# A four-layer decoder kernel on one core: its opening in another order, with zeros multiplied while the input is loaded

## The reference

```python
def _rmsnorm(x, g):
    return x * lax.rsqrt(jnp.mean(jnp.square(x), axis=-1, keepdims=True) + RMS_EPS) * g

def _mla(x, positions, w_dq, q_norm, w_uq, w_dkv, kv_norm, w_ukv, w_o):
    cq = _rmsnorm(x @ w_dq, q_norm)                     # 1024 -> 384
    q = (cq @ w_uq).reshape(b, s, h, NOPE + ROPE)       # rope on the last 64
    ckv = x @ w_dkv                                     # 1024 -> 256 + 64
    c_kv = _rmsnorm(ckv[..., :KV_LORA], kv_norm)
    k_pe = _rope(ckv[..., KV_LORA:], positions, theta)
    kv = (c_kv @ w_ukv)
    ...

# differential attention, second layer:
lam = exp(sum(lq1 * lk1)) - exp(sum(lq2 * lk2)) + lambda_init
```

## Time and profile before

| | us |
|---|---|
| median of 3 runs | 1593.34 |
| the runs | 1593.21 to 1595.19 |
| the profiled execution | 1595.48 |
| its span, first to last instruction | 1593.7 |

### The profile page before, as it was taken

The page is one execution under the profiler, slowest core; times in us unless marked ns, Lnnn a source line. Parts: engine busy times, 40 slices in busy tenths (PEclk is TensorE's granted clock), DMA queues, the critical chain, the costliest instruction groups (busy, mean ns, idle before and its releaser), DMA issues.

```text
span 1593.7 us, 20708 instructions
## 1 busy us (share of the span) xinstructions
PE 1557.3 (98%) x8570; PEld 1338.0 (84%) x8570; DVE 1077.0 (68%) x1390; ACT 752.9 (47%) x874; POOL 18.5 (1%) x77
## 2 busy tenths in 40 slices
PE   7999999999999999999999999999999999999997
PEld 6878888799888888888888888887888888788886
DVE  6777656868766567655777665577555868965557
ACT  4734444357254353544455254444444365444542
POOL 1000000000000000000000000000000000000000
PEclk9999999999999999999999999999999999999999
DMA  8446655553465565666474655546555562475551
GB/s 265 133 142 210 199 190 185 191 178 108 151 219 186 193 198 189 187 194 198 143 230 133 205 186 190 185 159 224 194 190 185 157 210 94 132 237 185 185 189 49
DMA packets 198444, 285.97 MB, mean 179 GB/s; under 512 B 9287, under 2 KB 167055, under 8 KB 198351
## 3 DMA queue, kind: packets, MB, share of 16 engines
q1 hardware_dynamic: 194943, 272.20, 52.6%
q0 software_dynamic: 3264, 11.93, 2.3%
q10 hardware_dynamic: 144, 0.52, 0.1%
HBM read 283.58 MB, written 1.05 MB: 179 GB/s over the span
## 4 chain that ended last, share of the span: by engine, by line
PE 81%; DVE 12%; ACT 3%; issue 1%; DMA 1%; SPq 0%; DVEq 0%; ACTq 0%
PE ps L397 39%; PE ps L426 25%; PE ps L430 13%; DVE wlo L293 2%; PE ps L449 2%; ACT whi L288 2%; DVE x L529 1%; DVE res L526 1%; DVE stats L503 1%; DVE res L500 1%; DVE xt L488 1%; DVE nt L518 1%; DMA raw<-in_mla_w_dq 1%; DMA raw<-in_w_in_mlstm 1%; PE ps L1577 1%
## 5 line engine op out<-in xcount | busy, mean ns | idle before, releaser
L293 DVE TENSOR_TENSOR wlo<-raw,whi 128x2048 fp32r<-128x2048 f32 (+2 forms) x259 | 576.7, 2256 | 232.6 <-ACT whi L288 231.4
L288 ACT ACTIVATE whi<-raw 128x2048 fp32r<-128x2048 f32 (+2 forms) x262 | 483.0, 1879 | 20.3 <-DMA raw<-in_w_in_mlstm 4.8
L397 PE MATMUL ps<-whi,yt 128*128 128x512 f32 (+1 forms) x1472 | 462.4, 387 | 1.7 <-DVE wlo L293 1.0
L426 PE MATMUL ps<-xt,whi 128*128 128x512 f32 x1728 | 431.8, 392 | 0.0
L426 PEld LDWEIGHTS ps<-xt,whi 128*128 128x128 f32 x1728 | 314.7, 189 | 58.2
L397 PEld LDWEIGHTS ps<-whi,yt 128*128 128x128 f32 x1472 | 275.5, 189 | 56.8 <-DVE wlo L293 2.3
L397 PE MATMUL ps<-wlo,yt 128*128 128x512 f32 (+1 forms) x736 | 284.4, 386 | 0.0
L430 PEld LDWEIGHTS ps<-xt,wlo 128*128 128x128 f32 x1728 | 235.8, 191 | 16.8
L430 PE MATMUL ps<-xt,wlo 128*128 128x256 f32 x1728 | 241.1, 283 | 0.0
L397 PE MATMUL ps<-whi,xt 128*128 128x512 f32 (+4 forms) x778 | 221.5, 363 | 3.6 <-DVE wlo L293 2.7
L721 ACT ACTIVATE arena<-ps 128x512 f32<-128x512 f32 x108 | 64.1, 594 | 285.1 <-PE ps L430 285.1
(11 more groups left out here) (229 smaller groups left out, 923.1 us busy)
## 6 DMA issues: line engine op xcount, KB each, us to landing
raw<-in_ffn_w_up SPq DMA_DIRECT2D x76, 1024.0 KB, 5.4
raw<-in_ffn_w_down SPq DMA_DIRECT2D x76, 1024.0 KB, 4.9
raw<-in_ffn_w_gate SPq DMA_DIRECT2D x44, 1024.0 KB, 5.3
raw<-in_diff_w_qkv SPq DMA_DIRECT2D x12, 1024.0 KB, 5.2
raw<-in_w_in_conv SPq DMA_DIRECT2D x10, 1024.0 KB, 5.3
raw<-in_w_out SPq DMA_DIRECT2D x8, 1024.0 KB, 4.9
raw<-in_w_in_mlstm SPq DMA_DIRECT2D x7, 1024.0 KB, 7.6
raw<-in_w_in_mlstm SPq DMA_DIRECT2D x8, 768.0 KB, 4.2
```

Of the source, the lines that this page charges most:

```text
L288: nc.scalar.activation(whi[:, u.slot, 0:u.size], raw[:, u.slot, 0:u.size], ACT.Copy).then_inc(w_hi[u.slot], 1)
L293: nc.vector.tensor_tensor(wlo[:, u.slot, 0:u.size], raw[:, u.slot, 0:u.size], whi[:, u.slot, 0:u.size].bitcast(F32), ALU.subtract).then_in ...
L397: m = nc.tensor.matmul(out_, p, q, start=first and n == 0, stop=last and n == 2, skip_group_check=True)
L426: nc.tensor.matmul(o.rearrange("p (a n) -> p a n", a=2), parts[c][0], xt2[:, :, c, :], start=c == 0, stop=False, skip_group_check=True)
```

## The change

1. GpSimd makes the identity first, then the ones and the rotary frequencies, then masks and the rest. It issues gb only after the high half of unit 3 has been made.
2. ScalarE's queue issues the four lambda rows and the positions, then x's second half. SP no longer issues them.
3. Unit 0 is loaded, split into its parts and waited for in two halves of two chunks each.
4. VectorE first writes a 128x128 tile of zeros; TensorE multiplies it by itself 14 times, then spreads lambda, then transposes x when it is there. VectorE makes lambda's sums, the rotary tables and lambda before it touches x; ScalarE makes the exponential, loads the sine's table by a dummy sine and makes the sines before it touches x. Both then do t = 0 of x, both halves of unit 0, t = 1 of x, and units 1 to 3.
5. In the first block VectorE takes the first root and scales the latents before it splits unit 4 (qp); it splits unit 5 (qn0) after the lows of the query latents instead of before them. TensorE transposes the query latents halfway through unit 3 instead of before it.

```diff
+        def load_first(sp, u):
+            for k, done in enumerate((first_loaded, w_loaded[u.slot])):
+                sp.dma_start(slot_view(raw, u)[:, 2 * k:2 * k + 2],
+                             u.src[:, 2 * k:2 * k + 2]).then_inc(done, 16)
+        def first_high(act, u, k):
+            act.wait_ge((first_loaded, w_loaded[u.slot])[k], 16)
+            nc.scalar.activation(whi[:, u.slot, first_half(u, k)], raw[:, u.slot, first_half(u, k)],
+                                 ACT.Copy).then_inc((first_hi, w_hi[u.slot])[k], 1)
+        def first_low(dve, u, k):
+            dve.wait_ge((first_hi, w_hi[u.slot])[k], 1)
...
                 for j, u in enumerate(group):
-                    wait_split(pe, u)
+                    if u is not dq[0]:
+                        wait_split(pe, u)
                     for t in range(TT):
                         for c in range(4):
                             if c == 0 and bank0 == 0:
                                 wait_x(pe, -1, t, j)
+                            if u is dkv[0] and t == 1 and c == 0:
+                                pe.wait_ge(lam_c, 1)
+                            if u is dkv[1] and t == 1 and c == 0:
+                                turn_latents(range(QC), 0)
+                            if u is dq[0] and t == 0 and c % 2 == 0:
+                                pe.wait_ge(w_lo[u.slot], 1 + c // 2)
...
                     if u is dq[0]:
                         params_tensor(pe)
-                    if u is dkv[0]:
-                        lambda_tensor(pe)
-                        turn_latents(range(QC), 0)
...
-            split.after(dq[0])
             roots(0, QL)
             for t in range(TT):
                 nc.vector.tensor_scalar(latent[:, t, 0:QL], ps[:, t, 0:QL], rs[:, t:t + 1],
                                         None, ALU.mult).then_inc(m_latent, 1)
+            split.after(dq[0])
+            lows(range(QC), (2, 2, 3))
             split.after(dq[1])
-            lows(range(QC), (2, 2, 3))
-            lambda_vector(dve, link)
             split.after(dkv[0])
             roots(TT, KVL)
...
         def start_gpsimd(pool):
-            load_gb(pool, 0)
-            nc.gpsimd.memset(ident[:, :], 0.0)
+            nc.gpsimd.memset(ident[:, :], 0.0).then_inc(ident_made, 1)
+            pool.wait_ge(ident_made, 1)
+            nc.gpsimd.affine_select(out=ident[:, :], in_=ident[:, :], compare_op=ALU.not_equal,
...
+        def start_small_loads(act):
+            for k, w in enumerate(("q1", "k1", "q2", "k2")):
+                act.dma_start(lam_rows[:, k, :], a[f"diff_lambda_{w}"]).then_inc(lam_loaded, 16)
             for t in range(TT):
...
+                act.dma_start(pos_i[:, t:t + 1], a["positions"][0, t * P:(t + 1) * P].rearrange(
+                    "(p a) -> p a", a=1)).then_inc(pos_loaded, 16)
 
         def start_tensor(pe):
-            pe.wait_ge(consts, 2)
+            pe.wait_ge(idle_made, 1)
+            for _ in range(IDLE_PRODUCTS):
+                nc.tensor.matmul(ps[:, 0, 0:P], idle, idle, start=True, stop=True,
+                                 skip_group_check=True)
+            lambda_tensor(pe)
+            pe.wait_ge(ident_made, 2)
...
         def start_scalar(act, split):
-            for t in range(TT):
-                for h in range(2):
-                    ln_high(act, -1, t, h)
-                split.to(0)
-            split.to(3)
             act.wait_ge(lam_s, 1)
             nc.scalar.activation(lam_e[:, :], lam_e[:, :], ACT.Exp).then_inc(lam_x, 1)
+            act.wait_ge(idle_made, 1)
+            nc.scalar.activation(exp_ready[:, :], idle[0:1, 0:1], ACT.Sin)
             act.wait_ge(rope_ang, 1)
...
+            for t in range(TT):
+                for h in range(2):
+                    ln_high(act, -1, t, h)
+                if t == 0:
+                    first_high(act, order[0], 0)
+                    first_high(act, order[0], 1)
+                    split.n = 1
             split.to(3)
+
+        def start_vector(dve, link, split):
+            nc.vector.memset(idle, 0.0).then_inc(idle_made, 1)
             dve.wait_ge(lam_loaded, 64)
...
             dve.wait_ge(consts, 1)
-            dve.wait_ge(row_loaded, 16 * N_ROW_DMAS)
+            dve.wait_ge(pos_loaded, 16 * TT)
...
+            lambda_vector(dve, link)
+            for t in range(TT):
+                for h in range(2):
+                    ln_low(dve, -1, t, h)
+                if t == 0:
+                    first_low(dve, order[0], 0)
+                    first_low(dve, order[0], 1)
+                    split.n = 1
+            split.to(3)
             dve.wait_ge(par_t, 1)
...
             start_gpsimd(pool)
+            pool.wait_ge(w_hi[3], 1)
+            load_gb(pool, 0)
...
+            start_small_loads(act)
             act.dma_start(x[:, 1, :], a["x"][0, P:S, :]).then_inc(x_loaded[1], 16)
```

More of the change, by code:

```diff
@@ L295, in split_lo, with first_half @@
                                     ALU.subtract).then_inc(w_lo[u.slot], 2)
+        def first_half(u, k):
+            return slice(k * u.size // 2, (k + 1) * u.size // 2)
+        def load_first(sp, u):
[8 more added lines that the diff above has]
+            dve.wait_ge((first_hi, w_hi[u.slot])[k], 1)
+            nc.vector.tensor_tensor(wlo[:, u.slot, first_half(u, k)], raw[:, u.slot, first_half(u, k)],
+                                    whi[:, u.slot, first_half(u, k)].bitcast(F32),
+                                    ALU.subtract).then_inc(w_lo[u.slot], 1)
         def split_half(dve, u, k):
@@ L329, in half @@
                 self.n += k
+        pos_loaded = sem("pos_loaded")
+        lam_c = sem("lam_c")
+        first_loaded = sem("first_loaded")
+        first_hi = sem("first_hi")
         row_loaded = sem("row_loaded")
@@ L2265, in build @@
         ang = sb("ang", [P, TT, 3, ROPE // 2 + ROT // 2])
+        idle = arena[:, ARENA - P:]
+        IDLE_PRODUCTS = 14
+        idle_made = sem("idle_made")
+        ident_made = sem("ident_made")
         lam_s = sem("lam_s")
@@ L2276, in start_gpsimd @@
         def start_gpsimd(pool):
-            load_gb(pool, 0)
-            nc.gpsimd.memset(ident[:, :], 0.0)
+            nc.gpsimd.memset(ident[:, :], 0.0).then_inc(ident_made, 1)
+            pool.wait_ge(ident_made, 1)
+            nc.gpsimd.affine_select(out=ident[:, :], in_=ident[:, :], compare_op=ALU.not_equal,
+                                    fill=1.0, base=0, pattern=[[-1, P]],
+                                    channel_multiplier=1).then_inc(ident_made, 1)
+            nc.gpsimd.memset(ones[:, :], 1.0)
+            for k, f in enumerate(freqs(10000.0, ROPE) + freqs(500000.0, ROT)):
+                m = nc.gpsimd.memset(rope_f[:, k:k + 1], float(f))
+            m.then_inc(consts, 1)
             nc.gpsimd.memset(masks[:, :, :], 0.0)
@@ L2281, in start_gpsimd @@
             nc.gpsimd.memset(sel[:, :, :], 0.0)
-            nc.gpsimd.memset(ones[:, :], 1.0)
             nc.gpsimd.memset(kvm[:, :, :, :], 0.0).then_inc(q_zero, 1)
[L2284 to L2289, removed]
+            pool.wait_ge(q_zero, 1)
             nc.gpsimd.affine_select(out=masks[:, 0, :], in_=masks[:, 0, :], compare_op=ALU.is_ge,
@@ L2316, in params_tensor @@
             pe.wait_ge(row_loaded, 16 * N_ROW_DMAS)
+            pe.wait_ge(consts, 2)
             wait_x(pe, -1, 1, 1)
@@ L2325, in lambda_tensor @@
             pe.wait_ge(lam_x, 1)
-            nc.tensor.matmul(ps[:, 7, 0:2], ones[0:1, 0:P], lam_e[:, :], start=True,
+            pe.wait_ge(consts, 1)
+            nc.tensor.matmul(ps[:, 3, 0:2], ones[0:1, 0:P], lam_e[:, :], start=True,
                              stop=True).then_inc(lam_b, 1)
         def start_scalar(act, split):
-            for t in range(TT):
-                for h in range(2):
-                    ln_high(act, -1, t, h)
-                split.to(0)
-            split.to(3)
             act.wait_ge(lam_s, 1)
             nc.scalar.activation(lam_e[:, :], lam_e[:, :], ACT.Exp).then_inc(lam_x, 1)
+            act.wait_ge(idle_made, 1)
+            nc.scalar.activation(exp_ready[:, :], idle[0:1, 0:1], ACT.Sin)
             act.wait_ge(rope_ang, 1)
@@ L2396, in lambda_vector @@
             dve.wait_ge(lam_b, 1)
-            nc.vector.tensor_copy(small[:, 62:64], ps[:, 7, 0:2]).then_inc(par_c, 1)
-            dve.wait_ge(par_c, 2)
+            nc.vector.tensor_copy(small[:, 62:64], ps[:, 3, 0:2]).then_inc(lam_c, 1)
+            dve.wait_ge(lam_c, 1)
             link(nc.vector.scalar_tensor_tensor(out=lam, in0=small[:, 63:64], scalar=LAMBDA_INIT,
@@ L2412, in _ @@
                     start_loads(sp)
-                load(sp, u)
+                if k == 0:
+                    load_first(sp, u)
+                else:
+                    load(sp, u)
             for t in range(TT):
```

10 lines of the change are left out of this document (1 added, 9 removed).

## The result

The changed kernel took 1597.24 us (median of 9 runs, 1596.16 to 1599.28), the kernel before 1593.59 in the same comparison (9 runs, 1592.65 to 1595.19). The ratio is 1.0025, its 95% interval 1.0015 to 1.0035: **slower by 3.65 us**. The forecast was 1592.5 with a range to 1596.0, so it was wrong, by its sign too.

A forecast was written before the change was run, and what follows sets the result against it. TensorE was taken to bound the kernel, busy 98%, with losses in its opening. A 3.1 us earlier second root minus 2.3 for the low clock gave 0.8 gained: 1594.7 profiled, 1592.5 at the median; range 1588.8 to 1596.0.

The forecast's parts named there:

- L: Landing of the positions at the start: 5.7 us, from a range of 4.5 to 7.2; first product 2.7 us earlier.
- x's second half: Its transfer, issued 2 us later, lands at 7.6 and is wanted only at about 10.5.
- L + 6.5: Start of TensorE's first product: 6.5 us after the positions land, at 12.2 instead of 14.93.
- Rival 3: Small transfers land late and hold VectorE's in-order queue: slower, 1596.8 with positions landing at 10; chance 0.10.
- c = 2.3: Loss to TensorE's low clock in w_dq's products: 2.3 us instead of 3.0, since the clock falls after the zeros.
- The queue: VectorE's new order between w_dq's end and the second root: 12.0 us instead of 9.45, so 2.5 us later.
- forecast gap of 4 us: TensorE waits 4 us before qn0 for the root's chain, against 1.0 us in two gaps before.
- Rival 2: Clock also falls in the new 4 us gap before qn0: 1.7 us more, 1594.2; chance 0.16.
- a shift left at qn0 reaches the end whole: Any shift left when qn0's products begin (41.20 us before) arrives at the kernel's end in full.
- The expected gain: Second root at 32.8 + c against 35.92, c being the low-clock loss of 2.3: 0.8 us gained.

The follow-up runs named there:

- e1: Changed kernel without the 14 products of zeros: 1597.94 us, ratio 1.0028.
- e2: Changed kernel with the old order of VectorE's queue and of the turned latents in the first block: 1593.90 us, ratio 0.9999.
- e9: Changed kernel plus 10 products of ones on TensorE between qp and the turning of the second latents: 1596.31 us, ratio 1.0016.
- e4: Changed kernel with the two transfers of positions issued ahead of the four lambda rows: 1595.10 us, ratio 1.0011.
- e13: Changed kernel with e2's old order and e4's issue order together: 1591.86 us, ratio 0.9993.
- e3: Changed kernel with x, unit 0 and units 1 to 3 ahead of lambda and the rotary tables on ScalarE and VectorE: 1596.41 us, ratio 1.0016.
- e6: e3 with e2's old order, and x's second half issued ahead of the small transfers: 1591.68 us, ratio 0.9991.
- e8: e7 with 8 zero products ahead of x's transposes instead of 14, and 3 behind each half: 1592.34 us, ratio 0.9995.
- e11: e10 plus 9 and 5 products of ones in TensorE's two waits: 1591.64 us, ratio 0.9990.
- e12: Kernel before plus 20 zero products ahead of x's transposes, 14 behind, and first root ahead of qp's low half: 1594.22 us, ratio 1.0006.
- e7: e6 with gb's transfers issued behind unit 7's high half instead of unit 3's: 1592.56 us, ratio 0.9994.
- e10: e8 with the first root ahead of qp's low half and the parameters turned inside w_dq's second unit: 1593.21 us, ratio 1.0001.

## Why the prediction was wrong

**L, the step that failed.** "Nearest row for the landing: x's second half, 4.9 us for 512 KB, which is the upper end: L = 7.2." It was no upper end. From issue to landing the positions took 6.40 in the profile after, 7.45 in e1, 8.08 in e2 and 8.13 in e9, so L is 9.0 to 10.7, and I had 5.7. The Trainium skill (DMA: Bandwidth & Descriptors, Anatomy of one DMA) gives its fixed part of about 2.0 us for the path of GpSimd's transfers, and these went out on ScalarE's queue; taken for them it is even further off, and the measurement decides. In e4 and e13, where the positions go out first, all six small ones are there by about 8. I took a small transfer, issued later, to be at most as slow as a large one that was issued first. (The middle between 4.5 and 7.2 is 5.9, not 5.7; that slip is small.) The next step held: L + 6.5 against 15.63 - 8.98 = 6.65, and 6.55 from the cast in all of after, e1, e2 and e9. Rival 3, to which I gave 0.10, was the case; at L = 10 it says 1596.8, and the median is 1597.24.

**x's second half** was to land at 7.6 "by its 4.9 us" and landed at 11.5. It was issued 2.3 us later, behind the small transfers and beside more weights. In the changed kernel that hides behind the positions; in e3 it is the bound.

**c = 2.3** was met: 6.52 - 4.2. Its reason, that the clock falls in the gap and the zeros are wasted, held (e1). The size was the middle of a range and luck: with a later first product it was smaller, 6.15 - 4.25 = 1.9 in e1 and e2, and with an earlier one larger, 7.10 - 4.24 = 2.9 in e13. In the trace after, TensorE was busy 1.80 of 3.30 us before the fall at 9.99, which lies inside its idle 3.10 us. This agrees with what the Trainium skill (TensorE: Matmul & The Clock Gate, HAM oscillation) says of idle gaps. In e4 the longest wait before the fall at qn0 was only 2.3 us.

**The queue** was to cost 2.5 and cost 1.84 (e2): the latents' lows ended 8.0 after w_dq, not 8.6. Sign and place were right: the forecast gap of 4 us with the turn of t = 0 in it is there, from 39.0 to 43.0. With L = 9.0 in my own sum the second root comes at 9.0 + 6.5 + 8.6 + 2.3 + 12.0 = 38.4, 2.5 late; it came at 37.76, 1.84 late. So **with the right L my sum gives 1592.5 + 3.3 = 1595.8**, and this one term accounts for 3.3 of the 4.7 us between forecast and median.

**Rival 2** is not seen in the changed kernel's own profile (4.32 us at qn0). Of the four profiles with the new queue and no filler (after, e1, e3, e4) one shows it, e4's, for 1.1 us where I had 1.7; of the eight with the old queue one does too, e6's. e9, which fills that gap, is 0.8 lower, and e2, which removes it, 1.6 lower than the order's 1.84 explains; neither proves that this clock is the reason. I had treated rivals 2 and 3 as alternatives, and nothing keeps them from adding. The 1.4 us between 1595.8 and the median stay open. An L later than the profiled 9.0 is one part that the traces support: against the kernel before, the profiles of after, e1 and e9 (L = 9.0, 10.0 and 10.7) are 2.2, 2.6 and 3.3 us late at 1259. The clock at qn0 and the one near 82 us (last section) are the others. Each profile shows one execution, and single runs of the kernel before spread over 4.7 us (1591.57 to 1596.27).

**That a shift left at qn0 reaches the end whole** holds only roughly. After qn0 (1.83) the profile after is 2.2 us late up to 1270 and 0.7 at the end: the profiled execution of the kernel before had a transfer of 9.37 us in its chain at 1278.49 which the other has not.

```profile
1278.49 9.37 DMA raw<-in_w_in_mlstm
```

And in e2 and e13 the products gain 1.3 on the kernel before between qn0 and the first layer norm (near 110), for the reason in the last section.

**The expected gain** would hardly have come from the start alone. e6 starts the products 5.4 us earlier, and 1.8 arrive in its median: parameter rows, tables ahead of the first root, w_uq and then w_o take the places of what was removed, and each new wait may bring the clock down.

## What to carry to other kernels

When an in-order engine gets a tiny transfer as its first wait, price the landing by a row of a tiny transfer issued in the same crowd, or put the range's end well above that of the big ones; better, issue it first or put work ahead of the wait. Warm-up products on TensorE brought nothing with a gap of 5 us behind them (e1 against the changed kernel), and nothing where VectorE's queue took up the gain (e12); so look first at what comes after them and at the engine behind TensorE. Low halves ahead of a reduction's root in VectorE's queue, with the latents turned later, cost 1.84 us even though TensorE had other products meanwhile, and after an emptier stretch the clock may be low, as in e4.

## What the runs showed of the hardware that I had not expected

The second of two transfers of 0.5 KB (128 pieces of 4 bytes each) took 6.4 to 8.1 us from 2.58 on, while x and the weights were under way (after, e1, e2, e3, e9), longer than 512 KB issued first (4.9). Issued at 1.19 it took 5.3 (e4). 512 KB issued at about 3.1 behind the six small ones took 8.4 to 9.6, and 6.8 in e4, where the same six stood ahead with the positions first; w_dq's second unit on the other queue took 9.1 to 11.6 in the former and 8.9 in the latter. Whether the small transfers or the crowd held x is not separated.

The clock falls after stretches in which TensorE is far from idle: 1.80 busy of 3.30 us (after), 2.14 of 4.40 (e4). One such stretch, in the attention near 82 us, brings it down in some profiled executions and not in others. Stretches of the kernel after, and of e2:

```profile
84.00:87.00 3.00, 2.50 (x9) 1.99 (x10) 1.37 (x6) 1.91 (x8) 0.00 (x0) 0.68 0.00 0
```

```profile
84.00:87.00 3.00, 2.87 (x16) 2.27 (x17) 2.11 (x6) 1.56 (x6) 0.00 (x0) 1.00 0.00 0
```

It is there in the profiles of the kernels before and after, e1, e3, e4, e6, e8, e9, e11 and e12, and missing in e2, e7, e10 and e13; in e2 and e13 its absence is the 1.3 us. All five profiles with the new queue in the first block have it (after, e1, e3, e4, e9), and five of the nine with the old order of it or most of it. So it may be chance, or the new queue may bring it about more often, which could be a part of e2's unexplained 1.6; one profile of each version can't tell. Either way one profile can be 1.3 us off its kernel, and differences of this size need the medians.
